# Halves for the first unit's homes, a new place for the second gate's rows, and column halves for the last unit's second matrices and adding store

## What is computed

```python
def hier_moe(h, p):
    B, L, D = h.shape
    t = h.reshape(B * L, D)
    g_logit = (t @ p['w_gr']).astype(F32) + p['b_gr'].astype(F32)
    ...
    top_v, top_i = lax.top_k(e_in, TOP_K)
    top_w = jax.nn.softmax(top_v, axis=-1) * g_w
    eid = g_sel[:, None] * EXP_PER_GROUP + top_i
    combine = jnp.einsum('tk,tke->te', top_w, jax.nn.one_hot(eid, N_EXPERTS, dtype=F32)).astype(h.dtype)
    a = jnp.einsum('td,edf->tef', t, p['w1'])
    u = jnp.einsum('td,edf->tef', t, p['w3'])
    y = jnp.einsum('tef,efd->td', jax.nn.silu(a) * u * combine[:, :, None], p['w2'])
    return y.reshape(B, L, D)
```

## Time and profile before

| | us |
|---|---|
| median of three runs | 1055.73 (1055.2 to 1056.48) |
| the profiled execution | 1053.14 |
| its span | 1051.3 |
| PE busy | 992.0 (94%) |
| DVE busy | 516.0 (49%) |
| POOL busy | 265.0 (25%) |
| ACT busy | 232.9 (22%) |
| chain that ended last: PE | 79% |
| chain that ended last: DMA | 10% |

### The profile page before, as it was taken

The page is one execution under the profiler, slowest core; times in us unless marked ns, Lnnn a source line. Parts: engine busy times, 40 slices in busy tenths (PEclk is TensorE's granted clock), DMA queues, the critical chain, the costliest instruction groups (busy, mean ns, idle before and its releaser), DMA issues.

```text
span 1051.3 us, 11753 instructions
## 1 busy us (share of the span) xinstructions
PE 992.0 (94%) x4332; PEld 590.7 (56%) x4332; DVE 516.0 (49%) x1018; ACT 232.9 (22%) x464; POOL 265.0 (25%) x268
## 2 busy tenths in 40 slices
PE   8899999999999999999999999999999998878785
PEld 6566656655555677777777777745584332322231
DVE  3378652255645345667667655537674321321223
ACT  3224330134555311111111111111112111211111
POOL 0333310011530133544465334200010211211101
PEclk9999999999999999999999999999989998998988
DMA  9735346000000271221311421275379999999995
GB/s 370 298 139 230 120 177 254 1 6 2 1 1 1 101 289 52 65 87 51 101 51 57 166 68 61 79 274 168 113 292 355 332 401 398 399 426 399 403 409 175
DMA packets 37625, 193.65 MB, mean 184 GB/s; under 512 B 7658, under 2 KB 12458, under 8 KB 27712
## 3 DMA queue, kind: packets, MB, share of 16 engines
q1 hardware_dynamic: 32800, 182.31, 45.1%
q0 software_dynamic: 4624, 10.06, 3.9%
q10 hardware_dynamic: 144, 0.52, 0.1%
HBM read 185.50 MB, written 14.09 MB: 190 GB/s over the span
## 4 chain that ended last, share of the span: by engine, by line
PE 79%; DMA 10%; SPq 3%; DVE 2%; issue 2%; ACT 2%; POOL 0%; POOLq 0%; DVEq 0%; ACTq 0%
PE psum L1110 23%; PE psum L867 8%; PE psum L1144 7%; PE psum L1186 7%; PE psum L1328 6%; DMA r_bv<-in_w_e 4%; PE psum L960 3%; PE psum L1344 3%; DMA r_w<-in_w_e 3%; PE psum L1044 3%; SPq L678 2%; PE psum L1060 2%; PE psum L812 2%; DMA r_w<-in_w_ada 2%; PE psum L1071 2%
## 5 line engine op out<-in xcount | busy, mean ns | idle before, releaser
L1110 PE MATMUL psum<-r_h,r_w 128*128 128x320 f32 x512 | 143.6, 433 | 0.0
L2604 POOL TENSOR_TENSOR r_w<-r_w 128x512 f32<-128x512 f32 x64 | 84.7, 1332 | 221.6 <-PE psum L1110 155.0
L1110 PEld LDWEIGHTS psum<-r_h,r_w 128*128 128x128 f32 x512 | 97.1, 190 | 40.6 <-issue 0.3
L1110 PE MATMUL psum<-r_ys,r_w 128*128 128x320 f32 x384 | 111.2, 432 | 0.0
L1110 PEld LDWEIGHTS psum<-r_ys,r_w 128*128 128x128 f32 x384 | 73.0, 190 | 30.4
L1613 ACT ACTIVATE r_bv<-r_bv 128x320 f32<-128x320 f32 x64 | 30.1, 470 | 238.8 <-DVE r_bv L2141 238.8
L2632 POOL DMA_INDIRECT out_y<-r_bv,tab x17 | 26.8, 1577 | 202.0 <-DVE r_bv L2405 202.0
L1186 PE MATMUL psum<-r_w,r_bv 128*128 128x512 f32 x160 | 72.2, 597 | 0.0
L2150 DVE TENSOR_TENSOR r_t<-psum,r_t 128x320 f32<-128x320 f32 x112 | 52.2, 483 | 9.3 <-PE psum L1144 8.0
L2127 DVE SCALAR_TENSOR_TENSOR r_t<-r_bv,r_t 128x320 f32<-128x320 f32 x48 | 46.8, 975 | 1.2 <-ACT r_bv L1613 1.2
L2141 DVE TENSOR_TENSOR sqbuf<-psum,r_bv 128x320 f32<-128x320 f32 x32 | 15.7, 492 | 64.4 <-PE psum L1110 64.4
(11 more groups left out here) (461 smaller groups left out, 2019.0 us busy)
## 6 DMA issues: line engine op xcount, KB each, us to landing
r_a<-in_w_ada SPq DMA_DIRECT2D x8, 2048.0 KB, 8.5
r_w<-in_w_gate SPq DMA_DIRECT2D x32, 512.0 KB, 4.6
r_a<-in_w_e SPq DMA_DIRECT2D x6, 2048.0 KB, 31.7
r_c<-in_w_e SPq DMA_DIRECT2D x5, 2048.0 KB, 31.2
r_c<-in_w_e SPq DMA_DIRECT2D x8, 1024.0 KB, 34.9
r_w<-in_w_e SPq DMA_DIRECT2D x4, 2048.0 KB, 34.3
r_ys<-in_w_e SPq DMA_DIRECT2D x4, 2048.0 KB, 36.4
r_bv<-in_w_e SPq DMA_DIRECT2D x4, 2048.0 KB, 36.6
```

Source lines behind the costliest of these rows:

```text
L1110: ins = mm(gate_bank(u, n), w[:, k, :], x[:, k, :], start=(k == 0), stop=(k == HK - 1))
L2604: g.tensor_tensor(w_mix[n], x, y, op).then_inc(s_wm, 1)
```

## The change

**First unit's homes by halves.** `W13_PIECES` is 2 for streams 6 and 7. PE counts `s_first` once more after the lower row blocks of unit 0; SP waits for that and issues the lower halves of w13 6 and 7, then, at `s_A` as before, the upper halves.

**Second gate's rows.** PE's order is now: products of unit 0, gate row 0, `pair_T(1)`, gate row 1, overflow table. ACT takes them in that order.

**Last unit.** Its w13 is loaded whole, one DMA for each expert, on the ordinary semaphore. Its w2 comes in column halves: columns 0 to 511 of both experts, then 512 to 1023 of both on `w2_rest`. PE projects the first column half, counts `s_Y`, waits for `w2_rest`, projects the second and counts again. DVE multiplies each half when it is there. POOL stores it by two adding DMAs on half rows, with the indices `last_rows` that DVE makes by two more instructions.

```diff
-W13_PIECES = [4 if 2 <= i < NBUF else 1 for i in range(len(STREAM))]
+W13_PIECES = [4 if 2 <= i < NBUF else 2 if i in (NBUF, NBUF + 1) else 1 for i in range(len(STREAM))]
...
+            def load_w2_columns(i, n, done):
+                halves = lambda w: w.rearrange("p (f n) -> p f n", f=2)[:, :, n * 512:(n + 1) * 512]
+                sp.dma_start(halves(wexp[i % NBUF][1]), halves(a["w_e"][STREAM[i][1], :, W13:EW])).then_inc(done, 16)
...
+                if u == 0:
+                    sp.wait_ge(s_first, TT + 1)
+                    for i in AFTER[0]:
+                        load_w13(i, (0,))
                 if AFTER[u]:
                     sp.wait_ge(s_A, u + 1)
                 for i in AFTER[u]:
-                    if i in AT[LAST]:
-                        load_piece(i, wexp[i % NBUF][0][:, 0:W13 // 2], 0, W13 // 2, w13_loaded[i % NBUF])
+                    if u == 0:
+                        load_w13(i, (1,))
                     else:
                         load_w13(i)
-                for i in AFTER[u]:
-                    if i in AT[LAST]:
-                        load_piece(i, wexp[i % NBUF][0][:, W13 // 2:W13], W13 // 2, W13, w13_rest)
                 if u and AFTER[u - 1]:
                     sp.wait_ge(s_Y, u)
                     for i in AFTER[u - 1]:
-                        load_w2(i)
+                        if i not in AT[LAST]:
+                            load_w2(i)
+                    for n, done in enumerate((w2_loaded, [w2_rest] * NBUF)):
+                        for i in AFTER[u - 1]:
+                            if i in AT[LAST]:
+                                load_w2_columns(i, n, done[i % NBUF])
...
-                hidden(H_SLOT[u % 2], halves, range(0, KD // 2))
+                ins = hidden(H_SLOT[u % 2], halves, range(0, KD // 2))
+                if u == 0:
+                    ins.then_inc(s_first, 1)
...
-                if u == LAST:
-                    pe.wait_ge(w13_rest, 16 * len(AT[LAST]))
...
+            pe.wait_ge(s_cntd, 2)
+            hidden_of(0)
             pe.wait_ge(s_lgd, TT)
             second_gate_row(0)
-            pe.wait_ge(s_cntd, 2)
-            hidden_of(0)
+            pair_T(1)
             pe.wait_ge(s_g2r, 1)
             second_gate_row(1)
-            pair_T(1)
...
+                    project(halves, Y_SLOT[u], (0,)).then_inc(s_Y, 1)
+                    pe.wait_ge(w2_rest, 16 * len(AT[LAST]))
+                    project(halves, Y_SLOT[u], (1,)).then_inc(s_Y, 1)
...
                 for n in range(2):
+                    if p == LAST:
+                        dve.wait_ge(s_Y, p + 1 + n)
...
-                ins.then_inc(s_yd, 1)
+                    if n or p == LAST:
+                        ins.then_inc(s_yd, 1)
...
+                half_rows = out["y"].rearrange("t (h n) -> (t h) n", h=2)
+                for h in range(2):
+                    pool.wait_ge(s_yd, u + 1 + h)
+                    pool.indirect_dma_start(half_rows, bass.IndirectOffsetOnAxis(ap=last_rows[:, h:h + 1], axis=0),
```

More of the change, by code:

```diff
@@ L337, in build @@
         xtab = sb("xtab", 3, I32)
+        last_rows = sb("last_rows", 2, I32)
         R = {}
@@ L466, in build @@
         s_h2d = sem("h2_stored")
-        s_first = sem("first_unit_rows_chosen")
+        s_first = sem("first_unit_rows_chosen_and_low_half_projected")
         s_g2f, s_g2r = sem("second_gate_rows_filled"), sem("second_gate_rows_ready")
@@ L490, in build @@
         w13_loaded = [sem(f"w13_loaded{i}") for i in range(NBUF)]
-        w13_rest = sem("last_w13_upper_rows_loaded")
+        w2_rest = sem("last_w2_upper_columns_loaded")
         w2_loaded = [sem(f"w2_loaded{i}") for i in range(NBUF)]
@@ L782, in _ @@
             overflow(sp, n_x, load_chunk)
-            sp.wait_ge(y_stored[0], 16 * (LAST // 2 + 1))
+            sp.wait_ge(y_stored[0], 16 * (LAST // 2 + 2))
             sp.wait_ge(y_stored[1], 16 * (LAST // 2))
@@ L1336, in hidden_T, with project @@
                 return ins
-            def project(halves, slot=2):
-                for n in range(2):
+            def project(halves, slot=2, ns=range(2)):
+                for n in ns:
                     for f in range(2):
@@ L1398, in _ @@
                 pe.wait_ge(s_hT, u + 1)
-                project([(lo, wexp[i % NBUF][1:], hT[:, u % 2, :, lo:lo + C]) for lo, i in zip((0, C), AT[u])], Y_SLOT[u]) \
-                    .then_inc(s_Y, 1)
+                halves = [(lo, wexp[i % NBUF][1:], hT[:, u % 2, :, lo:lo + C]) for lo, i in zip((0, C), AT[u])]
+                if u < LAST:
+                    project(halves, Y_SLOT[u]).then_inc(s_Y, 1)
+                else:
+                    project(halves, Y_SLOT[u], (0,)).then_inc(s_Y, 1)
+                    pe.wait_ge(w2_rest, 16 * len(AT[LAST]))
+                    project(halves, Y_SLOT[u], (1,)).then_inc(s_Y, 1)
                 if u == 2:
@@ L1690, in _, with take_second_gate_row @@
             take_pair_T(0)
-            for i in range(2):
+            def take_second_gate_row(i):
                 act.wait_ge(s_g2f, i + 1)
                 A(g2_row[:, i, :], psum[:, 2, :], ACT.Copy).then_inc(s_g2r, 1)
+            take_second_gate_row(0)
             take_pair_T(1)
+            take_second_gate_row(1)
             act.wait_ge(s_g2r, 2)
@@ L2331, in _ @@
             v.tensor_copy(pair_w[:, 0:PAIRS, :], filled_tab[:, :, 1:3]).then_inc(s_tab, 1)
+            for h in range(2):
+                v.tensor_scalar(last_rows[:, h:h + 1], filled_tab[:, TAB_COL[LAST], 0:1], 2.0, h - 2.0, ALU.mult, ALU.add)
             over9 = r_sq[:, 0:9 * NE].rearrange("p (n j) -> p n j", j=9)
@@ L2647, in put_rows @@
                 n = rows_of(u)
-                scatter(y_sb[0:n, u % 2, :], tab[0:n, TAB_COL[u], 0:1], y_stored[u % 2])
+                if u < LAST:
+                    scatter(y_sb[0:n, u % 2, :], tab[0:n, TAB_COL[u], 0:1], y_stored[u % 2])
+                    return
+                half_rows = out["y"].rearrange("t (h n) -> (t h) n", h=2)
+                for h in range(2):
+                    pool.wait_ge(s_yd, u + 1 + h)
+                    pool.indirect_dma_start(half_rows, bass.IndirectOffsetOnAxis(ap=last_rows[:, h:h + 1], axis=0),
+                                            y_sb[:, u % 2, h * 512:(h + 1) * 512], None, bounds_check=2 * NT - 1,
+                                            oob_is_err=False, compute_op=ALU.add).then_inc(y_stored[u % 2], 16)
             pool.wait_ge(s_wo, 2 * TT)
```

## The result

| | before | after |
|---|---|---|
| median of nine runs each | 1055.73 us | 1061.1 us |
| the profiled execution | 1053.14 us | 1059.22 us |
| its span | 1051.3 us | 1057.3 us |

The changed kernel is slower: the ratio of after to before is 1.0058, with a 95% interval of 1.004 to 1.0076. That is +6.1 us (4.2 to 8.0). By that ratio the time is 1061.9 us. The forecast was 1059.9 us, its range 1057.3 to 1062.4 us.

A forecast was written before the change was run, and what follows sets the result against it. The prediction took a saturated DMA stage, hanging on the w13 issue for unit 1 at 807.80 us, as the bound. Start +2.5 and tail +1.7 us gave +4.2 us on 1055.73: 1059.9 us, range 1057.3 to 1062.4 us.

The forecast's parts named there:

- Part 1: First unit's w13 homes by halves: costs 0, early bytes only lengthen the DMA engines' idle stretch before 807.80 us.
- Part 2: Second gate's rows reordered on PE: opened waits delay the issue at 807.80 us by 2.5 us (bounds 2.2 to 4.2).
- Wait (a): PE before unit 0's products: idle 1.13 us for ACT's copy of the first rows, which gate row 0 hid before.
- Step (c): PE before gate row 1: ACT's copy of gate row 0 is covered by the transposes but for 0.19 us.
- Step (d): PE before the overflow table's products: 1.2 us open wait for ACT's copy of row 1; products start 2.48 us later.
- the rival on the clock: At the table's products: the clock falls by the new wait, unit 1's products 1.7 us later still, 1061.6 us; chance 0.27.
- Part 3: Last unit's w13 whole: PE's first product there needs both whole matrices and starts 1.55 us later.
- Part 4: Last unit's w2 by column halves: saves nothing, since all of w2 lands before DVE's copy of the hidden values ends.
- Part 5: Two adding stores on POOL at the end: second starts 0.30 us after the first; landing at 1051.45 us against 1049.73 us.
- The start is not absorbed by the dip at 831 to 834 us: Rival at the DMA engines' later dip: it takes up 1.0 to 1.6 us of the start's shift, 1058.6 us; chance 0.10.
- Unit 0's release does not set the end: Rival at the first homes: unit 0's release sets the stage's end, so earlier lower halves gain, 1055.6 us; chance 0.10.
- The tail does not do what its titles say: Rival in the last unit: first column half stored while the second is projected, -1 us there, 1057.2 us; chance 0.08.

The follow-up runs named there:

- run 2: The kernel before with only the first unit's w13 homes (streams 6 and 7) given back by halves: ratio 1.0003 (0.9984 to 1.0023).
- run 9: The kernel before with unit 1 alone giving its w13 homes back by row halves, unit 0 whole: ratio 0.9972 (0.995 to 0.9993), 3.0 us faster.
- run 8: The kernel before with the w13 homes of the first two units (streams 6 to 9) given back by halves: ratio 0.9963, 3.9 us faster.
- run 4: The changed kernel with the gate rows put back in their old places on PE and ACT: ratio 1.0017 (1.0 to 1.0034) to before.
- run 3: The kernel before with only the last unit's parts: w13 whole, w2 by column halves, two adding stores: ratio 1.0017, +1.8 us.
- run 1: The kernel before with only the new order of the second gate's rows on PE and ACT: ratio 1.0037 (1.002 to 1.0054), +3.9 us.
- run 5: Run 1's kernel with one unread product of 512 columns more on PE, behind gate row 1: ratio 1.0022 to before, +2.3 us.
- run 7: The kernel before with w2 by column halves and two adding stores, last unit's w13 still in halves: ratio 1.0005 (0.998 to 1.003).
- run 6: The kernel before with the last unit's w13 loaded whole and nothing else: ratio 1.0018 (0.9995 to 1.0041), +1.9 us.

## Why the prediction was right, and where it was not

**What bounds the kernel: right.** It was said that the stage hangs on the issue for unit 1, not on that for unit 0. Runs 2 and 9 are the two sides of it: unit 0's homes by halves change nothing, unit 1's save 3.0 us (0.7 to 5.3). Over 799 to 840 us the DMA share, the clearest single row, reads before, after, in run 8 and in run 9:

```profile
799.00:840.00 41.00, 41.00 (x203) 15.35 (x202) 13.00 (x25) 8.26 (x13) 6.99 (x6) 1.00 0.97 339
```
```profile
799.00:840.00 41.00, 41.00 (x189) 15.41 (x191) 12.74 (x25) 8.26 (x13) 5.32 (x4) 0.93 0.81 271
```
```profile
799.00:840.00 41.00, 41.00 (x199) 14.71 (x200) 13.43 (x26) 8.26 (x13) 7.44 (x6) 1.00 1.01 358
```
```profile
799.00:840.00 41.00, 41.00 (x195) 14.47 (x194) 12.33 (x22) 7.88 (x12) 7.86 (x6) 0.98 1.01 350
```

From 840 to 1020 us all of them move 405 or 406 GB/s. The drop from 0.97 to 0.81 is worth 0.16 x 41 = 6.6 us of the engines' time; the rise from 0.97 to 1.01 is 1.6 us. The windows stand at fixed times, though the executions reach the last count up to 3.3 us apart; moved so that all begin at the same distance from it, they read 0.97, 0.81, 1.01 and 1.02.

**Part 1, cost 0: right** (run 2: 1.0003; run 4 against run 3).

**Part 2, +2.5 us: the steps were right, the term was too small.** Wait (a): 1.14 us for 1.13 us forecast. Step (c), row 1 behind the transposes: it starts 1.18 us behind their start, for 1.28 us. Step (d): 1.21 us for 1.2 us. The table's products start 14.57 us behind the last count, 2.39 us later than the 12.18 us of before (2.48 us forecast). What failed is what was set behind it: "all that follows, the issue at 807.80 us among it". The issue moved by 5.68 us, beyond this term's upper bound of 4.2 us, because the table's and unit 1's products ran at half clock. That is the rival on the clock, which had 0.27 and a price of 1.7 us. Its mechanism was the one to happen, in the profiles of after and of run 1. At the issue its price was mis-sized as well: 3.3 us by the rows of runs 1 and 5. In the times of these two runs it is 1.6 us. It was taken from a fall of 3.40 us; this one lasted 6.8 us. The argument against it, that the wait of 1.2 us is half of the 2.26 us of idle time in the earlier trace rows, did not hold: of two waits of 1.1 and 1.2 us with narrow products about them, the clock fell in both profiles.

**Part 3, +1.55 us: right, and incomplete.** From the issue for unit 1 to the last unit's first product the kernels with w13 whole take 219.4 to 219.8 us (four profiles), before takes 217.85 us: +1.5 to +1.9 us. (The other kernels that issue w13 8 whole and load the last w13 in halves, runs 1, 2, 5 and 7, take 215.2 to 217.0 us.) PE does wait for w13. The wait of 2.88 us brought a fall of the clock with it that was not in the sum, 1.74 us between first product and transposes. Yet run 6 measures 1.9 us and not 3.6 us in all. The profile of before is a favourable one to compare with. With w13 in halves PE enters the last unit earlier in runs 2, 5 and 7, but then waits inside it: 0.52 to 0.57 us for the upper halves, and 2.6 us before unit 15's second products (1030.31 us in run 7, where its last w2, in r_a, lands at 1030.3 us). In runs 5 and 7 the clock falls there for 3.4 us too. From the first product to the last unit's transposes these three take 14.4 to 16.0 us, where before takes 10.92 us. The steadier row goes from the issue for unit 1 to these transposes: 228.7 to 231.3 us in the five profiles with halves (before and runs 1, 2, 5 and 7), 232.0 to 232.5 us in the four with w13 whole. The means differ by 2.3 us, near the 1.8 and 1.9 us of runs 3 and 6. So the 1.74 us of the account are not a cost on top that the halves always avoid.

**Part 4: right.** PE projects the first column half when DVE's copy is there, w2 is complete 2.6 us before, and there is no wait between the halves. DVE's copy to the end of L2416 takes 1046.85 + 0.75 - 1043.16 = 4.44 us, as forecast, and the multiplication waits for DVE itself (0.20 us), not for PE. In run 8 the last w2 isn't what PE waits for either: it starts 1.15 us behind the transposes, on DVE's copy. In runs 1 and 2 it is, as before (a wait of 1.82 and 0.90 us).

**Part 5: right in form, a little too dear.** The second store is as long as the first (1.55 us) and 0.30 us behind it. Two sizes differ. The first store starts 1.20 us behind the first multiplication's end at 1048.49 us, where 0.79 us was forecast; that is 0.60 us behind the end of the second, so nearly all of the head start is gone. And from the end of the second store's instruction, 1053.10 us, it is 2.50 us to the landing, where 3.4 us was forecast and the whole store took 1049.70 - 1045.68 = 4.02 us (4.05 us in the prediction, from a rounded row). From the first multiplication's end to the last landing it is 7.11 us after and 1049.70 - 1042.74 = 6.96 us before: +0.15 us. The Trainium skill, "DMA: Bandwidth & Descriptors", section "Anatomy of one DMA — SWDGE (gpsimd) path", gives an estimate of 2.6 us for a half and 3.2 us for the whole (2.0 us, and bytes / 436e3). For the half it was nearer than my figure; for the whole the trace has 4.02 us and the measurement decides. That the second instruction on POOL uses up the saving was the prediction's own working; run 7 agrees with it (1.0005), though its interval can't tell 1 us from nothing.

**Why the number came out near.** The sum was +4.2 us, 6.1 us were measured, with a lower end of 4.2 us. By the times of the runs the parts are 2.3 us for the waits (run 5), 1.6 us for the clock (run 1 less run 5), 1.8 us for the tail (run 3) and 0.3 us for the first homes (run 2). So the waits and the tail were sized well, and the clock was left out of the sum. The ratio's 1061.9 us lies at the clock's rival, 1061.6 us, and not at the forecast; the range held because it was stretched to take that rival in. That its total fits to 0.3 us is in part luck, since at the issue the clock cost 3.3 us and not 1.7 us. In the times of whole runs the order costs 3.9 or 4.3 us and not 5.7 us. That would fit executions in which the clock falls for a shorter time, but only one of each kernel was profiled, so it stays open.

**The rivals that fell.** The start is not absorbed by the dip at 831 to 834 us: the dip moves with the issue for unit 1. Before has 169 GB/s in it, run 1 has 153 GB/s at 837 to 840 us, and run 2 has 153 GB/s at 825 to 828 us; and run 5's shift of 2.39 us gives 2.3 us in time. Unit 0's release does not set the end: run 2, and the DMA share before is 0.00 from 807.6 to 808.6 us, so no engine was still at work on the first homes there. The tail does not do what its titles say: run 3. And the rival that would have made it faster was a gain of the right kind in the wrong unit; it is unit 1's homes that had it.

## What to carry to other kernels

Where a stage keeps the DMA engines full to its end, find the last pause ahead of it and the release that ends that pause: the edit that gave nothing at the release before it (run 2) gave 3 to 4 us there (runs 8 and 9). Before work is moved out of a place where it covers a copy, price the wait that opens and also the clock behind it, which moved the next issue by more than the waits did here (3.3 us against 2.4 us), though by less in the times of the runs (1.6 against 2.3 us). A load in halves whose first half is just in time showed no wait in the profile of before, and 0.5 to 0.6 us in the middle in runs 2, 5, 7 and 8; making it whole opened one of 2.8 to 4.3 us at the start (runs 3, 4, 6 and after).

## What the hardware showed that was not expected

- The granted clock was at 0.5 for 6.8 us after a wait of 1.21 us, in both profiles with that wait open, while PE was busy all through these 6.8 us. The next issue came 3.3 us later for it. With one product of 512 columns in the wait it stayed at 1.00, in one profile.
- An adding store by indirect DMA takes POOL 1.55 us for 128 rows of 512 columns just as for 128 rows of 1024. Behind the instruction it is 2.5 to 2.6 us to the landing for the half size (after and runs 3, 4 and 7), 3.7 to 4.0 us for the whole (before and the other runs).
- The first large load behind the small table stores on SP (1.42 us for two) had a long issue in the profile of before: 5.62 us (819.79 us, r_bv). It is 5.5 to 5.8 us in all nine profiles in which unit 1's homes are given back whole. In run 8 it is 0.33 us, and 2.90 us for the next load; in run 9 it is 2.81 us. SP got there 34.13 us behind the last count in before and in run 8 alike, so it didn't start later there. Whether the table stores or the loads ahead of them hold it up wasn't tested.

```profile
819.79 5.62 SPq L678 DMA_DIRECT2D r_bv<-in_w_e  x1
```
```profile
818.63 0.33 SPq L678 DMA_DIRECT2D r_bv<-in_w_e  x1
819.00 2.90 SPq L678 DMA_DIRECT2D r_h<-in_w_e  x1
```

- Run 8 gains 3.9 us (1.7 to 6.2), where the DMA share gives 1.6 us. The shorter issue in the rows above may be a part of the rest. It wasn't tried apart, and stays open.
